# Up products of six FFNs: one 512-column matmul for the high weights, and the weight splits moved between the steps of the hidden part

## The chip, the cores and the metric

The kernel runs on one core of a Trainium2 chip. The metric is the device time of one execution in microseconds (us), as the median of the runs. TensorE (PE in the profile) multiplies, VectorE (DVE) and ScalarE (ACT) work elementwise, SyncE (SP) issues the DMAs. Every engine takes its own instructions in the order in which they are written, and waits on semaphores where one needs what another engine makes.

## The reference, cut to what matters

The program is a small network on 256 tokens of width 1024: two blocks with a mixer and a convolutional FFN each, then two layers with an FFN, a mixer and another FFN. The six FFNs are what the change touches:

```python
def swiglu(h, w_gate, w_up, w_down):
    return (jax.nn.silu(h @ w_gate) * (h @ w_up)) @ w_down
# second block, per layer i
mod = (cond @ w_mod[i] + b_mod[i]).reshape(-1, N_SUBLAYERS, 3, D_MODEL)
h = modulate(x, norm_g[i, 0], mod[:, 0, 0], mod[:, 0, 1])
x = x + FFN_RES_WEIGHT * mod[:, 0, 2][:, None, :] * swiglu(h, ...)
```

The first two FFNs are of another form (`conv_ffn`): the gate half goes through a depthwise convolution of three taps and a gelu before it multiplies the value half. Everything is float32.

## The kernel before, in words

**Precision by parts.** A float32 matrix product is made of three products of rounded operands: each operand is split into a high part (the value rounded to the type that TensorE takes, `fp32r`) and a low part (the rest), and high x high, high x low and low x high are summed. `PASSES` lists the three. A split of a weight piece of 128x1024 is a copy on ACT (high part) and a subtraction on DVE (low part).

**An FFN** (`ffn`, L942) walks over NF = 22 chunks j of 128 hidden channels. The weights of a chunk (two pieces for the up product, gate and value, and one for the down product, 1536 KB in all) come by one DMA into one of four ring slots (`weights`, `load`, L401). `split_up` (L986) splits the two up pieces into the buffer `wu[j % 2]`, `split_down` (L1010) splits the third and then gives the ring slot back. `up_zero` (L1092, chunk 0) and `pe_up` (L1111) make the up product: 2 halves x 8 k-steps x 3 passes = 48 matmuls of 256 columns (the 256 tokens) into one PSUM bank. `hidden` makes gate times value from it: in the plain FFNs silu (L1145, ACT), multiplication (L1172), high part (L1176), low part (L1177, DVE); in the convolutional ones a copy (L1150), the first tap (L1151), two more taps on DVE (L1157) and a gelu (L1166) stand in front. `pe_down` (L1127) multiplies the hidden chunk with the down weights: 12 matmuls of 512 columns.

**Order on TensorE**: up(j), down(j-1), up(j+1), down(j), ... without a gap in the code; down(j-1) waits for `hid[j-1]`, up(j) for the two up splits of chunk j and for the bank that chunk j-2 leaves.

**Modulation columns.** The vector `mod` (144 columns of 128 values) is computed along the way, beside the FFNs: for column c, 512 KB of `w_mod` come by DMA into one of four buffers (`mod_weights`, L981), DVE multiplies them with `crow` (`mod_products`, L1032), ACT sums over the row (`mod_sums`, L1043). When the sum of column c is made, its buffer is free, and the DMA of column c+4 is issued. `due` deals the columns out over chunks 2 to 21: the convolutional FFNs have 17 columns each (at most one in a chunk), the first plain FFN 38, the next two 36 each (two in most chunks, one in the others: 2 and 4 chunks of 20), the last none. The DMAs of weights and of columns stand in one queue, SP's.

**The loop** (`run`) writes, for chunk j: `weights(j+3)`, `split_up(j)`, `pe_up(j)`, `hidden(j-1)`, `mod_products(j)` (in the convolutional FFNs this stands inside `hidden`, after the taps), `mod_sums(j-1)`, `pe_down(j-1)`, `split_down(j)`. The product of column c thus stands behind `hidden(j-1)` on DVE, and the sum of it one turn later.

Of the kernel before, what the change touches and what calls it, by code (L numbers as in the profile page):

```python
# [246 lines left out]
def build(nc, dram, out, pat, cat):  # L247
    V, A, E, G = nc.vector, nc.scalar, nc.tensor, nc.gpsimd
    ctx = ExitStack()
    with ctx:  # L250
# [202 lines left out]
        PASSES = ((0, 0), (0, 1), (1, 0))  # L453
        THIRDS = ((0, slice(0, D)), (1, slice(0, 512)), (1, slice(512, D)))
# [487 lines left out]
        def ffn(name, gain, shift, conv=None, row=None, gate=None, mods=range(0)):  # L942
# [18 lines left out]
            hf = [htok_[:, 4 * T:5 * T]] * 2 if c3 else cv  # L961
            gp = [htok_[:, 5 * T + 4 + q * (T + 4):6 * T + 6 + q * (T + 4)] for q in range(2)]

            slot, up_split, down_split, up, down, mult, hid, mod_in, mod_prod = {}, {}, {}, {}, {}, {}, {}, {}, {}

# [17 lines left out]
            def split_up(j, free):  # L983
                s, full = slot[j]

                @block.scalar  # L986
                def _(_e):
                    A.wait_ge(*full)
                    for point in free:
                        A.wait_ge(*point)  # L990
                for g in range(2):
                    part = slice(g * CHUNK, (g + 1) * CHUNK)
                    raw = slot_ap(s, SLOT)[:, part]

                    @block.scalar
                    def _(_e):
                        Ring.p = act.count(A.activation(wu[j % 2][:, 0, part], raw, ACT.Copy).then_inc(act.sem, 1))  # L997

                    @block.vector
                    def _(_e):  # L1000
                        V.wait_ge(*full)
                        V.wait_ge(*Ring.p)
                        up_split[j, g] = dve.count(V.tensor_tensor(wu[j % 2][:, 1, part], raw, whole(wu[j % 2][:, 0, part]),  # L1003
                                                                   ALU.subtract).then_inc(dve.sem, 1))
# [76 lines left out]
            def up_zero(h_pts):  # L1081
# [3 lines left out]
                @block.tensor  # L1085
                def _(_e):
                    E.wait_ge(*up_split[0, 1])
                    for k in range(KC):
                        E.wait_ge(*h_pts[k])
                        for g in range(2):  # L1090
                            for n_, (wa, ha) in enumerate(PASSES):
                                ins = E.matmul(bank(4 + 2 * g)[:, 0:T], w[:, wa, g, k, :], h[:, ha, k, :],  # L1092
                                               start=k + n_ == 0, stop=k == KC - 1 and n_ == 2)
                    up[0] = pe.count(ins.then_inc(pe.sem, 1))

            def pe_up(j, row_point):

                w = wu[j % 2].rearrange("p a (c k n) -> p a c k n", c=2, k=KC)
                b = bank(4 + j % 2)

                @block.tensor
                def _(_e):
                    if j >= 2:
                        E.wait_ge(*mult[j - 2])
                    elif gate is not None:
                        E.wait_ge(*row_point)
                    for g in range(2):
                        E.wait_ge(*up_split[j, g])
                        for k in range(KC):
                            for n_, (wa, ha) in enumerate(PASSES):  # L1110
                                ins = E.matmul(b[:, g * T:(g + 1) * T], w[:, wa, g, k, :], h[:, ha, k, :],  # L1111
                                               start=k + n_ == 0, stop=k == KC - 1 and n_ == 2)
# [23 lines left out]
            def hidden(j, step):  # L1136

                z = j % 2
                gate_in = bank(4 + z)[:, 0:T]
                value = bank(6)[:, 0:T] if j == 0 else bank(4 + z)[:, T:2 * T]  # L1140
                if not c3:
                    @block.scalar
                    def _(_e):
                        A.wait_ge(*up[j])
                        Ring.p = act.count(A.activation(sg[z], gate_in, ACT.Silu).then_inc(act.sem, 1))  # L1145
                else:
                    @block.scalar
                    def _(_e):
                        A.wait_ge(*up[j])
                        al(A.activation(gp[z][:, 2:T + 2], gate_in, ACT.Copy).then_inc(act.sem, 1))  # L1150
                        Ring.p = act.count(A.activation(cv[z], gp[z][:, 0:T], ACT.Identity, scale=one(f"conv_w{conv}0", j),  # L1151
                                                        bias=one(f"conv_b{conv}", j)).then_inc(act.sem, 1))
                    for tap in (1, 2):
                        @block.vector
                        def _(_e):
                            V.wait_ge(*Ring.p)
                            Ring.p = dve.count(V.scalar_tensor_tensor(cv[z], gp[z][:, tap:tap + T], one(f"conv_w{conv}{tap}", j),  # L1157
                                                                      cv[z], ALU.mult, ALU.add).then_inc(dve.sem, 1))

                    tapped = Ring.p  # L1160
                    mod_products(step)

                    @block.scalar
                    def _(_e):
                        A.wait_ge(*tapped)
                        Ring.p = act.count(A.activation(sg[z], cv[z], ACT.Gelu_apprx_tanh).then_inc(act.sem, 1))  # L1166

                @block.vector
                def _(_e):
                    V.wait_ge(*Ring.p)  # L1170
                    V.wait_ge(*up[j])
                    mult[j] = vl(V.tensor_tensor(hf[z], sg[z], value, ALU.mult).then_inc(dve.sem, 1))  # L1172
                    if 2 <= j < NF - 1:
                        V.wait_ge(*down[j - 2, 1])
                    to = hr[z if j < NF - 1 else 2]
# [4 lines left out]
            def run(h_pts, nxt):  # L1180
# [17 lines left out]
                for j in range(1, NF):  # L1198
# [4 lines left out]
                    if j >= 2:  # L1203
# [2737 lines left out]
```

## Time and profile before

| | |
|---|---|
| median of 3 runs | 1964.86 us (1964.74 to 1965.02) |
| span of the profiled execution | 1963.3 us, first to last instruction; no device time of its own is shown for it |
| PE busy | 1866.7 us, 95% |
| DVE busy | 1426.9 us, 73% |
| ACT busy | 1174.4 us, 60% |
| PE's share of the chain that ended last | 83% |
| of it in up and down products of the FFNs (L1111, L1127, L1092) | 37% + 17% + 2% |

The FFNs lie at about 199 to 386 us, 571 to 758, 769 to 950, 1252 to 1440, 1446 to 1636 and 1770 to 1958. A row of the timeline gives start, duration and engine; "x48" means that so many instructions are merged into the row, and the duration runs from the first start to the last end. In brackets stands how long the engine was idle before it and who released it. The start of one row and of the next on the same engine give the pace; the end of a matmul is modelled and overlaps the next one.

### The profile page before, as it was taken

The page shows a single profiled execution, that of the slowest core. Times are in us where ns is not written, and L with a number is a line of the kernel's source. Part 1 is how long each engine was busy: PE and PEld are TensorE (multiplying, and loading weights), DVE is VectorE, ACT ScalarE, POOL GpSimd, SP SyncE. Part 2 cuts the span into 40 slices and gives each one's busy share as a digit, 9 for nine tenths or more (in the row PEclk, how much of TensorE's full clock was granted, in tenths as well). Part 3 has the DMA queues.
Part 4 walks back from the last instruction along what each step waited for, and adds up shares of the span by engine and source line. Part 5 has one row for each costly group of instructions (what it writes and reads, how often), then busy time and mean ns, then how long its engine had stood idle before and what let it go on. Part 6 is the DMA issues. An engine that isn't in the chain of part 4 may idle for free.

```text
span 1963.3 us, 36008 instructions
## 1 busy us (share of the span) xinstructions
PE 1866.7 (95%) x14638; PEld 1719.9 (88%) x14638; DVE 1426.9 (73%) x2196; ACT 1174.4 (60%) x2092; POOL 12.8 (1%) x25
## 2 busy tenths in 40 slices
PE   7898999898989999999999989999999999999998
PEld 7887999887779998999889967899989998879998
DVE  5687877764677777878778776878787787576555
ACT  6544666664666566666676675666666666575432
POOL 0000000020000000000000000000000000000000
PEclk9999999999999999999999999999999999999999
DMA  8304566354047664888444402588858883224551
GB/s 330 119 4 152 206 236 238 124 192 175 15 196 251 236 211 177 313 301 307 152 149 162 171 2 75 230 304 295 300 212 301 296 286 120 103 97 169 186 193 54
DMA packets 96357, 374.98 MB, mean 191 GB/s; under 512 B 5824, under 2 KB 6464, under 8 KB 95424
## 3 DMA queue, kind: packets, MB, share of 16 engines
q1 hardware_dynamic: 95552, 372.15, 52.5%
q8 instruction: 116, 1.90, 0.4%
q10 hardware_dynamic: 640, 0.52, 0.1%
q14 instruction: 49, 0.40, 0.1%
HBM read 371.08 MB, written 1.05 MB: 190 GB/s over the span
## 4 chain that ended last, share of the span: by engine, by line
PE 83%; DVE 9%; ACT 5%; issue 2%; ACTq 0%; DMA 0%; DVEq 0%; SPq 0%
PE psum L1111 37%; PE psum L1127 17%; PE psum L789 9%; PE psum L882 4%; PE psum L1092 2%; DVE buf L676 1%; PE psum L1742 1%; PE psum L3135 1%; PE psum L745 1%; DVE htok L3026 1%; PE psum L3594 1%; DVE x_res L535 1%; DVE htok L534 1%; PE psum L2628 1%; ACT buf L670 1%
## 5 line engine op out<-in xcount | busy, mean ns | idle before, releaser
L1111 PEld LDWEIGHTS psum<-buf,buf 128*128 128x128 f32 x6048 | 741.2, 192 | 8.9
L1111 PE MATMUL psum<-buf,buf 128*128 128x256 f32 x6048 | 744.4, 283 | 0.0
L1127 PE MATMUL psum<-buf,buf 128*128 128x512 f32 x1584 | 381.9, 391 | 0.0
L1127 PEld LDWEIGHTS psum<-buf,buf 128*128 128x128 f32 x1584 | 289.6, 188 | 55.4 <-DVE buf L1177 0.3
L1003 DVE TENSOR_TENSOR buf<-ring,buf 128x1024 fp32r<-128x1024 f32 x264 | 311.0, 1220 | 8.8 <-DVE modT L1059 7.5
L997 ACT ACTIVATE buf<-ring 128x1024 fp32r<-128x1024 f32 x264 | 263.3, 1046 | 0.0
L789 PE MATMUL psum<-buf,buf 128*128 128x256 f32 x1944 | 244.2, 285 | 7.8 <-DVE buf L676 7.3
L789 PEld LDWEIGHTS psum<-buf,buf 128*128 128x128 f32 x1944 | 236.4, 192 | 13.4 <-DVE buf L676 11.8
L1019 DVE TENSOR_TENSOR buf<-ring,buf 128x1024 fp32r<-128x1024 f32 x132 | 161.6, 1224 | 71.8 <-ACT buf L1014 71.8
L1014 ACT ACTIVATE buf<-ring 128x1024 fp32r<-128x1024 f32 x132 | 139.3, 1055 | 78.9 <-PE psum L1127 75.7
L1032 DVE TENSOR_TENSOR buf<-buf,crow 128x1024 f32<-128x1024 f32 x144 | 171.3, 1219 | 0.0
L1145 ACT ACTIVATE htok<-psum 128x256 f32<-128x256 f32 x88 | 33.7, 384 | 228.6 <-PE psum L1111 228.6
L676 DVE TENSOR_TENSOR buf<-ring,buf 128x1024 fp32r<-128x1024 f32 x97 | 119.0, 1235 | 69.7 <-ACT buf L670 62.5
L1043 ACT ACTIVATE buf<-buf 128x1024 f32<-128x1024 f32 x144 | 150.7, 1051 | 0.0
L1172 DVE TENSOR_TENSOR htok<-htok,psum 128x256 f32<-128x256 f32 x132 | 55.3, 419 | 122.6 <-ACT htok L1145 117.8
L882 PE MATMUL psum<-buf,buf 128*128 128x512 f32 x480 | 113.4, 393 | 1.9 <-DVE buf L866 1.0
L882 PEld LDWEIGHTS psum<-buf,buf 128*128 128x128 f32 x480 | 89.0, 188 | 22.0 <-DVE buf L866 1.7
L670 ACT ACTIVATE buf<-ring 128x1024 fp32r<-128x1024 f32 x97 | 101.7, 1053 | 7.2 <-issue 4.1
L1157 DVE SCALAR_TENSOR_TENSOR htok<-htok,params 128x256 f32<-128x256 f32 x88 | 42.6, 485 | 55.5 <-ACT htok L1151 53.9
L602 PE MATMUL psum<-early,htok 128*128 128x128 f32 x160 | 31.9, 357 | 37.8 <-DVE small L585 37.1
L1150 ACT ACTIVATE htok<-psum 128x256 f32<-128x256 f32 x44 | 16.9, 383 | 84.3 <-PE psum L1111 84.3
L3026 DVE SCALAR_TENSOR_TENSOR htok<-htok,params 128x256 f32<-128x256 f32 x128 | 61.9, 484 | 6.8 <-ACT htok L3018 3.3
(431 smaller groups left out, 2017.9 us busy)
## 6 DMA issues: line engine op xcount, KB each, us to landing
ring<-in_w_ffn SPq DMA_DIRECT2D x88, 1536.0 KB, 6.8
buf<-in_w_mod SPq DMA_DIRECT2D x144, 512.0 KB, 4.5
ring<-in_w_conv SPq DMA_DIRECT2D x44, 1536.0 KB, 6.6
ring<-in_w_ssd_in SPq DMA_DIRECT2D x16, 1536.0 KB, 6.6
ring<-in_w_ns_in SPq DMA_DIRECT2D x7, 1536.0 KB, 6.6
ring<-in_w_hy_in SPq DMA_DIRECT2D x6, 1536.0 KB, 14.8
ring<-in_w_ssd_out SPq DMA_DIRECT2D x5, 1536.0 KB, 6.7
ring<-in_w_cmp SPq DMA_DIRECT2D x4, 1024.0 KB, 5.2
```

The costliest lines, as they stand in the source:

```text
L670: Ring.p = act.count(A.activation(parts[:, 0, :], raw, ACT.Copy).then_inc(act.sem, 1))
L676: Ring.p = dve.count(V.tensor_tensor(parts[:, 1, :], raw, whole(parts[:, 0, :]), ALU.subtract).then_inc(dve.sem, 1))
L789: ins = E.matmul(b[:, 0:T], w[:, wa, k, :], h[:, ha, k, :], start=k + n_ == 0, stop=k == KC - 1 and n_ == 2)
L882: ins = E.matmul(acc[:, t, h * 512:(h + 1) * 512], self.parts[:, la, k % 4, t * P:(t + 1) * P], self.wp[self.turns[k]][wa][:, h * 512:(h + ...
L997: Ring.p = act.count(A.activation(wu[j % 2][:, 0, part], raw, ACT.Copy).then_inc(act.sem, 1))
L1003: up_split[j, g] = dve.count(V.tensor_tensor(wu[j % 2][:, 1, part], raw, whole(wu[j % 2][:, 0, part]), ALU.subtract).then_inc(dve.sem, 1))
L1014: Ring.p = act.count(A.activation(wd[j][:, 0, :], raw, ACT.Copy).then_inc(act.sem, 1))
L1019: down_split[j] = dve.count(V.tensor_tensor(wd[j][:, 1, :], raw, whole(wd[j][:, 0, :]), ALU.subtract).then_inc(dve.sem, 1))
L1032: mod_prod[c] = dve.count(V.tensor_tensor(w, w, crow[:, :], ALU.mult).then_inc(dve.sem, 1))
L1043: Ring.mod_last = act.count(A.activation(w, w, ACT.Copy, accum_out=modT[:, c:c + 1]).then_inc(act.sem, 1))
L1111: ins = E.matmul(b[:, g * T:(g + 1) * T], w[:, wa, g, k, :], h[:, ha, k, :], start=k + n_ == 0, stop=k == KC - 1 and n_ == 2)
L1127: ins = E.matmul(acc[:, t, g * 512:(g + 1) * 512], hr[z][:, ha, t * P:(t + 1) * P], wd[j][:, wa, g * 512:(g + 1) * 512], start=j == 0 and ...
```

## The change

1. `both_parts` (new): for each k-step the high weights are loaded once and multiply high and low part of the input in one matmul of 512 columns, which fills a whole bank; a second matmul of 256 columns adds low weights x high input to the bank's second half. It replaces three matmuls of 256 columns in chunks 0 to 20. Chunk 21 keeps the three passes. Gate and value have a bank each now, so two chunks take banks 4 to 7.
2. `sum_parts` (new): ACT copies the second halves of both banks (128x512) to SBUF, DVE adds the first halves (128x512) to it. Silu or the taps read the sum.
3. The high part of the hidden chunk is made by ACT (a copy to `hr`) in place of DVE's cast.
4. `split_up` for chunk j+1 is no longer one block in front of `pe_up`: its halves are dealt out inside `hidden(j-1)`, and `split_down(j)` stands inside it too.
5. `mod_products(j)` stands in front of `hidden(j-1)` for all FFNs.

```diff
+        def both_parts(b, w_high, w_low, h, k):
+            E.matmul(b.rearrange("p (a t) -> p a t", a=2), w_high, h[:, :, k, :], start=k == 0, stop=False)
+            return E.matmul(b[:, T:2 * T], w_low, h[:, 0, k, :], start=False, stop=k == KC - 1)
...
+            def sum_parts(j):
+                z = j % 2
+                high, low = (psum[:, 4 + 2 * z:6 + 2 * z, a * T:(a + 1) * T] for a in range(2))
+                @block.scalar
+                def _(_e):
+                    A.wait_ge(*up[j])
+                    if j >= 2:
+                        A.wait_ge(*mult[j - 2])
+                    low_part[j] = act.count(A.activation(up_sums[z], low, ACT.Copy).then_inc(act.sem, 1))
+                @block.vector
+                def _(_e):
+                    V.wait_ge(*low_part[j])
+                    up_sum[j] = dve.count(V.tensor_tensor(up_sums[z], high, up_sums[z], ALU.add).then_inc(dve.sem, 1))
...
+            def hidden(j, after):
+                sum_parts(j)
+                if j + 2 < NF:
+                    split_half(j + 2, 0, [up[j]])
+                if c3:
+                    conv_taps(j, up_sum[j])
+                    split_down(j + 1, after)
+                    activate(j, cv[z], tapped[j])
+                else:
+                    activate(j, up_sums[z][:, 0, :], up_sum[j])
+                # DVE: mult[j] = activated * value
...
+                if c3:
+                    if j + 2 < NF:
+                        split_half(j + 2, 1, [up[j]])
+                else:
+                    split_down(j + 1, after)
+                # ACT: high part of the product; DVE: low part, hid[j]
...
+                if not c3 and j + 2 < NF:
+                    split_half(j + 2, 1, [up[j]])
...
-                    if j >= 2:
-                        split_up(j, [up[j - 2]])
                     pe_up(j, row_point)
-                    hidden(j - 1, j)
-                    if not c3:
-                        mod_products(j)
+                    mod_products(j)
+                    hidden(j - 1, [] if j == NF - 1 else [down[j - 2, 1]] if j >= 2 else [h_pts[-1]])
                     mod_sums(j - 1)
```

In the rows of the order that follow, `buf_50` is the column buffer, `buf_136` and `buf_137` are the two up-split buffers, `buf_14x` the down splits, `buf_16x` the hidden parts; branches are left out.

DVE, third FFN, a chunk with two columns, before:

```order
L1003 TENSOR_TENSOR buf_136<-ring,buf_136 128x1024 [waits act_done,slot_full2]
L1003 TENSOR_TENSOR buf_136<-ring,buf_136 128x1024 [waits act_done,slot_full2]
L1172 TENSOR_TENSOR htok<-htok,psum 128x256 [waits pe_done,act_done]
L1176 CAST buf_161<-htok 128x256 [waits pe_done,dve_done]
L1177 TENSOR_TENSOR buf_161<-htok,buf_161 128x256 [waits dve_done]
L1032 TENSOR_TENSOR buf_50<-buf_50,crow 128x1024 [waits mod_full2]
L1032 TENSOR_TENSOR buf_50<-buf_50,crow 128x1024 [waits mod_full3]
L1019 TENSOR_TENSOR buf_142<-ring,buf_142 128x1024 [waits act_done]
```

And after the change:

```order
L1041 TENSOR_TENSOR buf_50<-buf_50,crow 128x1024 [waits mod_full0]
L1041 TENSOR_TENSOR buf_50<-buf_50,crow 128x1024 [waits mod_full1]
L1161 TENSOR_TENSOR hT<-psum,hT 128x512 [waits act_done]
L1008 TENSOR_TENSOR buf_136<-ring,buf_136 128x1024 [waits act_done,slot_full0]
L1202 TENSOR_TENSOR htok<-htok,hT 128x256 [waits act_done]
L1028 TENSOR_TENSOR buf_143<-ring,buf_143 128x1024 [waits act_done]
L1219 TENSOR_TENSOR buf_160<-htok,buf_160 128x256 [waits act_done]
L1008 TENSOR_TENSOR buf_136<-ring,buf_136 128x1024 [waits act_done,slot_full0]
L1041 TENSOR_TENSOR buf_50<-buf_50,crow 128x1024 [waits mod_full2]
L1041 TENSOR_TENSOR buf_50<-buf_50,crow 128x1024 [waits mod_full3]
```

The two column products (L1032, now L1041) stood behind the hidden part; now they stand directly ahead of the sum (L1161) with which the hidden part of chunk j-1 begins.

ACT, the same FFN, before:

```order
L1014 ACTIVATE buf_142<-ring 128x1024 [waits pe_done]
L997 ACTIVATE buf_137<-ring 128x1024
L997 ACTIVATE buf_137<-ring 128x1024
L1145 ACTIVATE htok<-psum 128x256 [waits pe_done]
L1043 ACTIVATE buf_50,modT<-buf_50 128x1024 [waits dve_done]
L1043 ACTIVATE buf_50,modT<-buf_50 128x1024 [waits dve_done]
```

And after the change:

```order
L1156 ACTIVATE hT<-psum 128x512 [waits dve_done,pe_done]
L1002 ACTIVATE buf_137<-ring 128x1024 [waits pe_done,slot_full3]
L1184 ACTIVATE htok<-hT 128x256 [waits dve_done]
L1023 ACTIVATE buf_142<-ring 128x1024 [waits pe_done]
L1214 ACTIVATE buf_161<-htok 128x256 [waits pe_done,dve_done]
L1002 ACTIVATE buf_137<-ring 128x1024 [waits pe_done,slot_full3]
L1052 ACTIVATE buf_50,modT<-buf_50 128x1024 [waits dve_done]
L1052 ACTIVATE buf_50,modT<-buf_50 128x1024 [waits dve_done]
```

The two row sums (L1043, now L1052), which release the DMAs of the columns four further on, stood right behind the silu; now they are the last work of the turn, behind a down split, the copy of the hidden part and the second up split.

## Rows read from the trace of the kernel before

**Rows 1.** The page's first part: busy time, share of the span, instructions.
```profile
PE 1866.7 (95%) x14638; PEld 1719.9 (88%) x14638; DVE 1426.9 (73%) x2196; ACT 1174.4 (60%) x2092; POOL 12.8 (1%) x25
```

**Rows 2.** The page's costliest groups: the matmuls of the FFN products, idle before them last.
```profile
L1111 PE MATMUL psum<-buf,buf 128*128 128x256 f32 x6048 | 744.4, 283 | 0.0
L1127 PE MATMUL psum<-buf,buf 128*128 128x512 f32 x1584 | 381.9, 391 | 0.0
```

**Rows 3.** Timeline, chunks of the first FFN: start, duration, engine, line, count, [idle before].
```profile
252.92 2.91 PE L1127 MATMUL psum<-buf,buf 128*128 128x512 f32 x12
253.12 0.39 ACT L1150 ACTIVATE htok<-psum 128x256 f32<-128x256 f32 x1 [2.10 <-PE psum L1111]
...
255.67 5.92 PE L1111 MATMUL psum<-buf,buf 128*128 128x256 f32 x48
...
261.42 0.86 PE L1127 MATMUL psum<-buf,buf 128*128 128x512 f32 x3
```

**Rows 4.** Timeline, one chunk of the third FFN, two modulation columns in it.
```profile
832.31 1.05 ACT L1043 ACTIVATE buf<-buf 128x1024 f32<-128x1024 f32 x1
...
833.35 1.05 ACT L1043 ACTIVATE buf<-buf 128x1024 f32<-128x1024 f32 x1
833.47 1.37 SPq L981 DMA_DIRECT2D buf<-in_w_mod  x2
833.57 2.35 DVE L1032 TENSOR_TENSOR buf<-buf,crow 128x1024 f32<-128x1024 f32 x2
...
835.74 1.99 ACT L997 ACTIVATE buf<-ring 128x1024 fp32r<-128x1024 f32 x2
...
837.01 2.35 DVE L1003 TENSOR_TENSOR buf<-ring,buf 128x1024 fp32r<-128x1024 f32 x2
837.12 0.38 SPq L401 DMA_DIRECT2D ring<-in_w_ffn  x1
...
842.07 2.35 DVE L1032 TENSOR_TENSOR buf<-buf,crow 128x1024 f32<-128x1024 f32 x2
```

**Rows 5.** DMAs of modulation weights in the first FFN, issue to landing.
```profile
DMA to landing us min/median/max: 3.4/3.5/4.2
```

**Rows 6.** The same in the third FFN.
```profile
DMA to landing us min/median/max: 3.8/4.9/6.5
```

**Rows 7.** Groups by line and shape: operations like the added ones.
```profile
L1157 DVE SCALAR_TENSOR_TENSOR htok<-htok,params 128x256 f32<-128x256 f32 x88 | 42.6, 485 | 55.5 <-ACT htok L1151 53.9
...
L1166 ACT ACTIVATE htok<-htok 128x256 f32<-128x256 f32 x44 | 18.4, 419 | 49.2 <-DVE htok L1157 49.2
...
L3768 ACT ACTIVATE htok<-psum 128x512 f32<-128x512 f32 x16 | 8.8, 619 | 3.7 <-PE psum L3757 3.7
...
L1912 DVE TENSOR_TENSOR buf<-buf,psum 128x512 f32<-128x512 f32 x10 | 6.9, 688 | 3.4 <-PE psum L1742 3.4
```

**Rows 8.** Timeline, start of the first FFN.
```profile
204.66 5.92 PE L1111 MATMUL psum<-buf,buf 128*128 128x256 f32 x48
204.94 1.06 ACT L1014 ACTIVATE buf<-ring 128x1024 fp32r<-128x1024 f32 x1 [1.18 <-DVE htok L1189]
...
206.03 1.22 DVE L1019 TENSOR_TENSOR buf<-ring,buf 128x1024 fp32r<-128x1024 f32 x1 [1.28 <-ACT buf L1014]
```

**Rows 9.** Timeline, start of the third FFN.
```profile
775.07 5.92 PE L1111 MATMUL psum<-buf,buf 128*128 128x256 f32 x48
...
776.90 1.22 DVE L1019 TENSOR_TENSOR buf<-ring,buf 128x1024 fp32r<-128x1024 f32 x1 [1.83 <-ACT buf L1014]
```

**Rows 10.** Windows: length, busy time of each engine, granted clock, DMA share, GB/s.
```profile
204.00:386.00 182.00, 182.00 (x1279) 170.86 (x1278) 141.51 (x204) 112.80 (x172) 0.00 (x0) 1.00 0.59 211
774.00:950.00 176.00, 176.00 (x1256) 166.34 (x1255) 141.27 (x174) 110.70 (x163) 0.00 (x0) 1.00 0.83 292
514.00:519.00 5.00, 3.04 (x26) 2.23 (x23) 4.30 (x10) 2.95 (x11) 0.00 (x0) 1.00 0.00 0
519.00:522.40 3.40, 3.40 (x16) 3.30 (x17) 1.47 (x4) 3.03 (x11) 0.00 (x0) 0.50 0.00 0
```

More of the change, by code:

```diff
@@ L1090, in _ @@
                         for g in range(2):
-                            for n_, (wa, ha) in enumerate(PASSES):
-                                ins = E.matmul(bank(4 + 2 * g)[:, 0:T], w[:, wa, g, k, :], h[:, ha, k, :],
-                                               start=k + n_ == 0, stop=k == KC - 1 and n_ == 2)
+                            ins = both_parts(bank(4 + g), w[:, 0, g, k, :], w[:, 1, g, k, :], h, k)
                     up[0] = pe.count(ins.then_inc(pe.sem, 1))
@@ new lines, in conv_taps, with _ @@
+            def conv_taps(j, point):
+                z = j % 2
+                @block.scalar
+                def _(_e):
+                    A.wait_ge(*point)
+                    Ring.p = act.count(A.activation(cv[z], gp[z][:, 0:T], ACT.Identity, scale=one(f"conv_w{conv}0", j),
+                                                    bias=one(f"conv_b{conv}", j)).then_inc(act.sem, 1))
+                for tap in (1, 2):
+                    @block.vector
+                    def _(_e):
+                        V.wait_ge(*Ring.p)
+                        Ring.p = dve.count(V.scalar_tensor_tensor(cv[z], gp[z][:, tap:tap + T], one(f"conv_w{conv}{tap}", j),
+                                                                  cv[z], ALU.mult, ALU.add).then_inc(dve.sem, 1))
+                tapped[j] = Ring.p
@@ L1142, in _, with hidden_last @@
+            def hidden_last(j):
+                z, to = j % 2, hr[2]
+                gate_in, value = (bank(4 + 2 * z + g)[:, 0:T] for g in range(2))
+                if c3:
                     @block.scalar
@@ L1144, in _ @@
                         A.wait_ge(*up[j])
[L1145 to L1166 removed]
+                        A.wait_ge(*mult[j - 2])
+                        Ring.p = act.count(A.activation(gp[z][:, 2:T + 2], gate_in, ACT.Copy).then_inc(act.sem, 1))
+                    conv_taps(j, Ring.p)
+                    activate(j, cv[z], tapped[j])
+                else:
+                    activate(j, gate_in, up[j])
                 @block.vector
                 def _(_e):
[L1170 removed]
+                    V.wait_ge(*activated[j])
                     V.wait_ge(*up[j])
                     mult[j] = vl(V.tensor_tensor(hf[z], sg[z], value, ALU.mult).then_inc(dve.sem, 1))
[L1173 to L1175 removed]
                     vl(V.tensor_copy(to[:, 0, :], hf[z]).then_inc(dve.sem, 1))
```

76 lines of the change are left out of this document (48 added, 28 removed).

## The prediction

> **What bounds the kernel now.** Read first the busy times: TensorE works 95% of the span, DVE 73%, ACT 60% [rows 1]. Then the groups of the FFN matmuls: 6048 of 256 columns and 1584 of 512, with no idle time before either [rows 2]. Then two timelines. In the first FFN one down product starts at 252.92, the up product at 255.67, the next down product at 261.42 [rows 3]: a turn of 8.50 us, 5.75 for 48 matmuls (0.120 each) and 2.75 for 12 (0.229 each), and nothing between. In the third FFN the two column products start at 833.57 and again at 842.07, the same 8.50 [rows 4]. So TensorE alone sets the pace of all six FFNs, and DVE and ACT follow with room. The question is whether they still do when their order is changed.
>
> The view that decides is again the timeline of the third FFN, read for one buffer [rows 4]: the row sums on ACT start at 832.31 and 833.35, the two column DMAs (one merged row) begin at 833.47, the products that need them start at 842.07. Between issue and use lie 7 to 8 us, and a landing takes 4.9 in the median there [rows 6]. That distance is what the change removes.
>
> **TensorE's part.** Three matmuls of 0.120 become one of 512 and one of 256 columns: 0.229 + 0.120 = 0.349 in place of 0.360. Per chunk 16 x 0.349 = 5.58 in place of 5.75: 0.17 us gained, in 21 chunks of each FFN 3.6 us, where TensorE still sets the pace. The 512-column price is that of the down product, whose input is contiguous; here it is two stretches of 256. I take it at the same price, the nearest row. The bounds are 0.240 (twice a matmul of 256, no gain) and 0.218 (twice the 0.109 that 256 further columns add between the two rows): 0 to 0.35 us a chunk, so over the 63 chunks of three FFNs in which TensorE still sets the pace 0 to 22 us, where I take 11.
>
> The row gives 0.120 for 256 columns at the full clock. The Trainium skill (TensorE: Matmul & The Clock Gate, "Wait — 56ns, not 53.3ns?") has start to start as columns over 2.4 GHz plus about 2.5 ns, 109 ns for 256 columns; by it a merged pair saves 2.5 ns, 0.04 us a chunk, and the total would come out some 9 us higher. The trace disagrees on the level (120, not 109), and I go by the trace.
>
> **What is added outside.** ACT copies 128x512 from PSUM: 0.62, the price of L3768; DVE adds 128x512 with PSUM: 0.69, that of L1912 [rows 7]. The high part of the hidden chunk goes from DVE to ACT (0.42, as L1166). As a load this is bearable: two DVE instructions of 128x1024 start 1.13 apart (2.35 for two of 1.22 [rows 4]), so DVE has per turn of a plain FFN five of these (three splits, two columns), 5.65, the sum 0.60, product and low part 0.33 each: 6.9 us of 8.33 (5.58 + 2.75). Between the two bounds (none hidden, 1.3 us a turn, 160 us; all hidden) I take all hidden as far as load goes, since TensorE needs the hidden part only a turn later.
>
> **The new loop, in the three FFNs with 36 or 38 columns.** DVE now takes the products of chunk j ahead of the sum of chunk j-1, and ACT makes the row sums last in the turn. The product of column c+4 waits for a DMA that waits for the row sum of column c, and with two columns a chunk that sum stands at the end of the turn just before. Everything of the hidden part is queued behind the waiting product on DVE: sum, splits, multiplication, low part; down(j-1) waits for them. Laid out from the start of the sum (0):
> - sum 0.69; the first up split starts at 0.60, the multiplication at 1.73 and ends at 2.15 (the silu, from 0.73, is long done).
> - ACT: high part from 2.19, second up split from 2.52, first row sum from 3.46 (two ACT copies of 128x1024 take 1.99, so they start 0.95 apart [rows 4]). From a row sum's start to its DMA 1.16 (832.31 to 833.47), the second 1.04 later [rows 4]: DMAs at 4.62 and 5.66.
> - Landing: 3.4 to 4.2, median 3.5, where the queues are little loaded [rows 5], 4.9 where they are at 83% [rows 6, 10]. The longer turn takes load away, and the 1536 KB of weights, which go out right behind the columns (now at 837.12, after a wait for the down split [rows 4]), have nine us to land. I take 3.6 for the first, 3.8 for the second.
> - First product at 8.27, second at 5.66 + 3.8 + 0.05 = 9.51, next sum 1.13 later: a turn of 10.64.
> - Where only the first of the two DMAs is waited for (a chunk with one column lies between, which shifts the distance), the product starts at 8.27 and the turn is 9.40.
>
> TensorE needs 8.33 of such a turn; it waits ahead of down(j-1), for the low part. Against 8.50 before, a full turn costs 2.14, a partial one 0.90. Dealing out the columns: the first two chunks with columns use the DMAs issued ahead; of the other 18 chunks of the 38-column FFN 14 turns are full and 4 partial, of each 36-column FFN 8 and 10. So 30 x 2.14 + 24 x 0.90 = 64.2 + 21.6 = 85.8 us. The slack of the first such turn (the low part would be ready some 2.5 us early) is lost again at the end, where the last down products follow each other without an up product between; I enter neither. The bounds of this term: zero if the wait never comes last; with every landing at the 4.9 of rows 6, 1.1 more per full and 1.3 more per partial turn, 33 + 31 = 64 us more; with 3.4 for all, some 14 less.
>
> The Trainium skill (DMA: Bandwidth & Descriptors, "Anatomy of one DMA") has a fixed part of about 2.0 us and 436 GB/s behind it, written for GpSimd's path: 3.2 us for 512 KB, an estimate. By it the total would be some 24 us lower. The shortest landing in these rows is 3.4, so I stay above.
>
> **The starts.** up(1) is over 5.58 after its start, and down(0) has no other product ahead of it. First FFN: up(1) starts at 204.66, DVE takes the down split of chunk 0 from 206.03 [rows 8]; the sum can start at 207.16, then split, two taps (0.48 each [rows 7]), down split, multiplication, and split and low part behind it: 0.60 + 1.13 + 1.0 + 1.13 + 0.33 + 1.13 + 0.43 = 5.75, ready at 212.9, against 210.2: 2.7 lost, in two FFNs. Third FFN: 775.07 and 776.90 [rows 9]; the sum from 778.03, then 0.60 + 1.13 + 0.33 + 1.13 + 0.43 = 3.6, ready at 781.65 against 780.65: 1.0 lost, in four FFNs. In the convolutional FFNs there is at most one column a chunk, so column c+4 is due four or more chunks after c, and the loop doesn't close. Their later turns stay with TensorE: DVE has 4 x 1.13 + 0.60 + 1.0 + 0.66 = 6.8 of 8.33.
>
> **Sum.** Loops +85.8; starts 2 x 2.7 + 4 x 1.0 = +9.4; gain 3 x 3.6 in the two convolutional FFNs and the last = -10.8; 3 x 3 chunks ahead of the loops x 0.17 = -1.5. Together +82.9: 1963.3 + 82.9 = 2046.2 us of span. The median of the runs is 1.6 above the profiled span; so 2048.
>
> **Rivals.**
> - Faster: the loop never closes, because the columns' data are there before DVE asks, and only the starts remain: 6 x 3.6 = 21.6 less, 9.4 more: 1963.3 - 12.2 + 1.6 = 1953. For it: 7 to 8 us between issue and use now [rows 4]. Against: the order on both engines, which leaves less than nothing of them. It decides from landings under 1.5 us, where a full turn (6.84 plus the landing) falls below TensorE's 8.33. Chance 0.09.
> - Slower still: the landings stay at 4.9, as in this FFN now [rows 6], because the weights and the second column share the queues: 2048 + 64 = 2112. Chance 0.08.
> - The clock: in a full turn TensorE stands for 10.64 - 8.33 = 2.3 us. Before, a stretch with 3.04 busy of 5.00 us was followed by 3.40 at clock 0.50, that is 1.2 GHz [rows 10]. One such stretch in a turn costs 1.7 of TensorE's time, inside the 2.3, so nothing. If the clock stays low, a turn needs 16.7, 6.0 and 7.3 over the two turns: 30 x 6.0 + 24 x 7.3 = 355 more, 2400. The Trainium skill (same TensorE page, "HAM oscillation") warns of exactly such waits between bursts; the stretch in rows 10 agrees, at a lower busy share than here. Chance 0.03.
> - In between, the loops closing less tightly (the sums earlier on ACT than laid out): 1965 to 2015, chance 0.06.
>
> **Numbers.** The forecast has 0.74. Range 2015 to 2090: the short landings below, half-way to the long ones above; what is left out is the faster case, the clock, half of the long landings and part of the in-between. A change within 0.2% (3.9 us, about what a measurement of this kernel can tell from none) has 0.02, faster by more 0.10, slower by more 0.88.
>
> **What would show it.** Right: in the third FFN DVE idle ahead of L1041 released by the DMA, about 2 us a turn; TensorE idle ahead of the down product, near 2.3 and 1.1; turns of 10.6 and 9.4; up products of 5.58; landings near 3.6; the convolutional and the last FFN shorter by 1 to 3 us each. Wrong: turns of 8.3 in the third FFN, or DVE waiting elsewhere; up products still at 5.75.

## The result, and the profile after

The changed kernel takes 2114.38 us (median of 4 runs, 2105.75 to 2119.56) against 1964.8: ratio 1.0756 with the interval 1.0738 to 1.0773, slower by 149.6 us. The forecast was 2048 with a range of 2015 to 2090: right in direction and place, too small by 66 us, and outside the range. The rival with the long landings had 2112. Ratios leave out one run, the one of ten of experiment 1 that took 2080.0 us at a granted clock of 0.842.

The page of the changed kernel (busy times, chain by line, and three groups of matmuls beside the column product), to be held against [rows 1, 2]:

```profile
PE 1907.4 (90%) x12622; PEld 1640.4 (78%) x12622; DVE 1468.4 (70%) x2196; ACT 1271.4 (60%) x2302; POOL 12.8 (1%) x25
...
DMA buf<-in_w_mod 12%; PE psum L457 10%; PE psum L1137 9%; PE psum L795 8%; PE psum L458 5%; ACT buf L1052 4%; DVE buf L1008 4%; PE psum L888 4%; ACT buf L1002 3%; DVE hT L1161 2%; DVE buf L682 1%; PE psum L751 1%; PE psum L1803 1%; DVE buf L1028 1%; DVE htok L1202 1%
...
L457 PE MATMUL psum<-buf,buf 128*128 128x512 f32 x2016 | 720.1, 400 | 3.0 <-DVE buf L627 2.9
L458 PE MATMUL psum<-buf,buf 128*128 128x256 f32 x2016 | 566.7, 281 | 0.0
L1137 PE MATMUL psum<-buf,buf 128*128 128x512 f32 x1584 | 420.1, 418 | 102.2 <-DVE buf L1219 100.3
...
L1041 DVE TENSOR_TENSOR buf<-buf,crow 128x1024 f32<-128x1024 f32 x144 | 175.6, 1223 | 213.1 <-DMA buf<-in_w_mod 210.1
```

TensorE has less to do in instructions (12622 matmuls for 14638) and stands idle ahead of the down product for 102 us, where before it never stood [rows 2]. DVE stands ahead of the column product for 213 us, 210 of them released by the columns' DMA, and this DMA has 12% of the chain. The list of who waited for whom (total, times, longest) names the links of one loop:

```profile
ACT htok L1184 <- DVE hT L1161: 280.5, 66, 7.4
DVE buf L1041 <- DMA buf<-in_w_mod: 210.1, 84, 4.6
...
PE psum L1137 <- DVE buf L1219: 100.3, 53, 4.3
```

One full turn of the fifth FFN, in its timeline (compare [rows 4]):

```profile
1699.83 1.04 ACT L1052 ACTIVATE buf<-buf 128x1024 f32<-128x1024 f32 x1
...
1700.10 5.49 PE L1137 MATMUL psum<-buf,buf 128*128 128x512 f32 x12 [4.03 <-DVE buf L1219]
...
1700.87 1.04 ACT L1052 ACTIVATE buf<-buf 128x1024 f32<-128x1024 f32 x1
1700.98 1.37 SPq L990 DMA_DIRECT2D buf<-in_w_mod  x2
...
1702.40 0.43 SPq L401 DMA_DIRECT2D ring<-in_w_ffn  x1
1704.66 1.23 DVE L1041 TENSOR_TENSOR buf<-buf,crow 128x1024 f32<-128x1024 f32 x1 [3.42 <-DMA buf<-in_w_mod]
...
1707.80 1.22 DVE L1041 TENSOR_TENSOR buf<-buf,crow 128x1024 f32<-128x1024 f32 x1 [1.91 <-DMA buf<-in_w_mod]
...
1708.95 0.68 DVE L1161 TENSOR_TENSOR hT<-psum,hT 128x512 f32<-128x512 f32 x1
...
1710.68 0.42 DVE L1202 TENSOR_TENSOR htok<-htok,hT 128x256 f32<-128x256 f32 x1
...
1711.13 0.42 ACT L1214 ACTIVATE buf<-htok 128x256 fp32r<-128x256 f32 x1
...
1712.21 0.42 DVE L1219 TENSOR_TENSOR buf<-htok,buf 128x256 fp32r<-128x256 f32 x1
1712.40 1.04 ACT L1052 ACTIVATE buf<-buf 128x1024 f32<-128x1024 f32 x1
...
1712.68 2.55 PE L1137 MATMUL psum<-buf,buf 128*128 128x512 f32 x10 [1.04 <-DVE buf L1219]
...
1713.56 1.37 SPq L990 DMA_DIRECT2D buf<-in_w_mod  x2
```

Read it from the row sums: ACT sums at 1699.83 and 1700.87, the column DMAs go out from 1700.98, the weights at 1702.40; DVE waits 3.42 us for the first column and 1.91 for the second; its sum (L1161) starts at 1708.95. Counted from there, the multiplication starts 1.73 later, the high part 2.18, the next row sum 3.45 and the next column DMA 4.61 later. The forecast had 1.73, 2.19, 3.46 and 4.62. The engines' part of the loop was right to 0.01 us. TensorE waits ahead of both down products (4.03 and 1.04).

What was wrong is one landing. The DMAs of the two columns in this turn, issued at 1700.98 and 1702.02, first and second:

```profile
L990 SPq DMA_DIRECT2D buf<-in_w_mod x1: 328/328/328, 1701.0 to 1701.0; - x1
...
DMA to landing us min/median/max: 3.7/3.7/3.7
```

```profile
L990 SPq DMA_DIRECT2D buf<-in_w_mod x1: 328/328/328, 1702.0 to 1702.0; - x1
...
DMA to landing us min/median/max: 5.8/5.8/5.8
```

Over the three FFNs 46 pairs of columns 1 us apart land in 3.69 us (first) and 5.56 us (second) in the mean; the forecast had 3.6 and 3.8. By the forecast a full turn is 6.84 plus the landing of the second, so 12.40 with this mean. From one DVE sum (L1161) to the next, as the forecast laid it out, 30 turns are above 10.7, 12.41 in the mean, and each of the 30 is the landing of its own second column plus 6.82 or 6.83. From one down product's start to the next, as turns are given in what follows, those above 10.7 have 12.28.

Windows over the third and the fifth FFN, one down product of the third, and the last FFN (length, busy, granted clock, DMA share and GB/s as in [rows 10]):

```profile
772.02:1020.50 248.48, 204.78 (x984) 168.52 (x985) 157.46 (x187) 136.45 (x217) 0.00 (x0) 0.93 0.61 212
1552.51:1780.73 228.22, 199.27 (x983) 165.40 (x984) 154.67 (x185) 134.55 (x213) 0.00 (x0) 0.95 0.63 221
863.20:866.60 3.40, 3.40 (x9) 2.64 (x9) 0.16 (x1) 2.34 (x4) 0.00 (x0) 0.51 0.73 193
1919.12:2105.00 185.88, 184.71 (x983) 158.03 (x984) 111.87 (x140) 93.66 (x137) 0.00 (x0) 1.00 0.43 153
```

The granted clock is at its lower level, 1.2 GHz, in stretches of the down products that follow a wait (0.51 in the third row); in the last FFN, with no columns, it is at 2.4 GHz throughout (1.00).

### The profile page after: what moved, and what is told of

Same layout as the page of the kernel before. It is cut to its first block, busy times and chain, and to the rows that moved or that the text cites. A ratio compares the mean times of both kernels' runs of the same rounds, so it can differ in the third digit from the quotient of the medians.

```text
span 2110.8 us, 32184 instructions
## 1 busy us (share of the span) xinstructions
PE 1907.4 (90%) x12622; PEld 1640.4 (78%) x12622; DVE 1468.4 (70%) x2196; ACT 1271.4 (60%) x2302; POOL 12.8 (1%) x25
## 4 chain that ended last, share of the span: by engine, by line
PE 50%; DVE 18%; ACT 13%; DMA 12%; issue 6%; ACTq 0%; DVEq 0%; SPq 0%
DMA buf<-in_w_mod 12%; PE psum L457 10%; PE psum L1137 9%; PE psum L795 8%; PE psum L458 5%; ACT buf L1052 4%; DVE buf L1008 4%; PE psum L888 4%; ACT buf L1002 3%; DVE hT L1161 2%; DVE buf L682 1%; PE psum L751 1%; PE psum L1803 1%; DVE buf L1028 1%; DVE htok L1202 1%
## 5 line engine op out<-in xcount | busy, mean ns | idle before, releaser
L457 PE MATMUL psum<-buf,buf 128*128 128x512 f32 x2016 | 720.1, 400 | 3.0 <-DVE buf L627 2.9
L458 PE MATMUL psum<-buf,buf 128*128 128x256 f32 x2016 | 566.7, 281 | 0.0
L1137 PE MATMUL psum<-buf,buf 128*128 128x512 f32 x1584 | 420.1, 418 | 102.2 <-DVE buf L1219 100.3
L457 PEld LDWEIGHTS psum<-buf,buf 128*128 128x128 f32 x2016 | 381.9, 189 | 99.0 <-DVE buf L627 6.2
L1137 PEld LDWEIGHTS psum<-buf,buf 128*128 128x128 f32 x1584 | 307.8, 201 | 186.7 <-DVE buf L1219 117.9
L458 PEld LDWEIGHTS psum<-buf,buf 128*128 128x128 f32 x2016 | 383.2, 190 | 5.0
L1008 DVE TENSOR_TENSOR buf<-ring,buf 128x1024 fp32r<-128x1024 f32 x264 | 321.4, 1221 | 20.2 <-ACT buf L1002 19.2
L1041 DVE TENSOR_TENSOR buf<-buf,crow 128x1024 f32<-128x1024 f32 x144 | 175.6, 1223 | 213.1 <-DMA buf<-in_w_mod 210.1
L1002 ACT ACTIVATE buf<-ring 128x1024 fp32r<-128x1024 f32 x264 | 275.5, 1049 | 0.0
L795 PE MATMUL psum<-buf,buf 128*128 128x256 f32 x1944 | 245.5, 286 | 7.5 <-DVE buf L682 7.1
L795 PEld LDWEIGHTS psum<-buf,buf 128*128 128x128 f32 x1944 | 237.7, 193 | 13.1 <-DVE buf L682 11.6
L1184 ACT ACTIVATE htok<-hT 128x256 f32<-128x256 f32 x84 | 34.9, 415 | 280.5 <-DVE hT L1161 280.5
L1028 DVE TENSOR_TENSOR buf<-ring,buf 128x1024 fp32r<-128x1024 f32 x132 | 161.8, 1225 | 28.2 <-ACT buf L1023 26.5
L1023 ACT ACTIVATE buf<-ring 128x1024 fp32r<-128x1024 f32 x132 | 139.0, 1053 | 48.5 <-PE psum L1137 45.5
L682 DVE TENSOR_TENSOR buf<-ring,buf 128x1024 fp32r<-128x1024 f32 x97 | 118.6, 1231 | 69.8 <-ACT buf L676 62.6
L1156 ACT ACTIVATE hT<-psum 128x512 f32<-128x512 f32 x126 | 74.0, 587 | 134.8 <-PE psum L458 132.5
L1052 ACT ACTIVATE buf<-buf 128x1024 f32<-128x1024 f32 x144 | 150.1, 1044 | 0.0
L1161 DVE TENSOR_TENSOR hT<-psum,hT 128x512 f32<-128x512 f32 x126 | 86.7, 688 | 87.0 <-ACT hT L1156 87.0
L888 PE MATMUL psum<-buf,buf 128*128 128x512 f32 x480 | 113.3, 393 | 1.9 <-DVE buf L872 1.0
L888 PEld LDWEIGHTS psum<-buf,buf 128*128 128x128 f32 x480 | 89.0, 188 | 21.9 <-DVE buf L872 1.7
L676 ACT ACTIVATE buf<-ring 128x1024 fp32r<-128x1024 f32 x97 | 101.6, 1053 | 6.9 <-issue 3.8
```

The costliest lines, as they stand in the source:

```text
L457: E.matmul(b.rearrange("p (a t) -> p a t", a=2), w_high, h[:, :, k, :], start=k == 0, stop=False)
L458: return E.matmul(b[:, T:2 * T], w_low, h[:, 0, k, :], start=False, stop=k == KC - 1)
L682: Ring.p = dve.count(V.tensor_tensor(parts[:, 1, :], raw, whole(parts[:, 0, :]), ALU.subtract).then_inc(dve.sem, 1))
L795: ins = E.matmul(b[:, 0:T], w[:, wa, k, :], h[:, ha, k, :], start=k + n_ == 0, stop=k == KC - 1 and n_ == 2)
L888: ins = E.matmul(acc[:, t, h * 512:(h + 1) * 512], self.parts[:, la, k % 4, t * P:(t + 1) * P], self.wp[self.turns[k]][wa][:, h * 512:(h + ...
L1023: Ring.p = act.count(A.activation(wd[j][:, 0, :], raw, ACT.Copy).then_inc(act.sem, 1))
```

## The experiments

All times are against the kernel before on the same chip, 1964.6 to 1965.1.

**1. The products behind the hidden part again.**

```diff
                     pe_up(j, row_point)
-                    mod_products(j)
+                    if c3:
+                        mod_products(j)
                     hidden(j - 1, [] if j == NF - 1 else [down[j - 2, 1]] if j >= 2 else [h_pts[-1]])
+                    if not c3:
+                        mod_products(j)
```

> The changed kernel with one edit: in the plain FFNs the column products stand behind the hidden part on DVE again, as before the change; all else of the change stays. Theory (a closed loop: row sum, column DMA, product, sum, hidden part, row sum, holds the three FFNs with 36 or 38 columns): the loop has a whole turn more of slack, the waits of DVE for the column DMAs (210 us in the changed kernel) go to nearly nothing, every FFN turn is 8.39 us, and the time falls by some 155 us to 1955-1963, a little below the kernel before. Rival (it is the added load on DVE and ACT, or the clock that falls to half, that makes the turns long): the time stays above 2050.

Measured: 1965.66 us, ratio 1.000 (0.9984 to 1.0016). A turn of the third FFN:

```profile
855.27 1.37 SPq L990 DMA_DIRECT2D buf<-in_w_mod  x2
...
855.59 2.36 DVE L1041 TENSOR_TENSOR buf<-buf,crow 128x1024 f32<-128x1024 f32 x2
...
857.33 2.91 PE L1137 MATMUL psum<-buf,buf 128*128 128x512 f32 x12
```

DVE takes the two products right after their predecessor, without a wait, and TensorE starts the down product without one. The turns of the plain FFNs are 8.39, but for a first one of up to 8.49. The loop is the whole loss: with the rest of the change in place, this one place is worth 149 us. The time is 3 us above the expected stretch, so of the gain of the shorter turns nothing is left; experiment 6 looks for it.

**2. The weights held back behind the columns.** `weights(j + 3)` stands behind `mod_products(j)` and its DMA waits for the last of two products:

```diff
+                        if len(due[j]) == 2:
+                            Ring.used[Ring.n % RING] = Ring.used[Ring.n % RING] + [mod_prod[due[j][-1]]]
+                        weights(j + 3)
```

> The changed kernel with one edit: where a chunk has two modulation columns, the 1536 KB DMA of weights for chunk j+3 is issued only when the products of these columns are done, so it no longer goes out 0.4 us behind the second column's DMA. The loop stays closed. Theory (the second column lands late, in 4.8 to 7 us, because the weights share the queues; that is the part of the forecast that was too small): the second landing comes down to 3.6-3.9 us, full turns from about 12.6 to 10.7, partial turns stay at 9.4-9.5, and the time is 2050-2065. Rival (the long full turns come from the half clock in the down products, or from the loop's ACT and DVE part): the landings get shorter but the turns stay above 12, and the time stays above 2095.

Measured: 2102.21 us, ratio 1.0695 (1.0679 to 1.0711). The expectation was missed; the time speaks for the rival, the landings say why:

```profile
1688.11 1.37 SPq L990 DMA_DIRECT2D buf<-in_w_mod  x2
...
1692.87 2.49 DVE L1041 TENSOR_TENSOR buf<-buf,crow 128x1024 f32<-128x1024 f32 x2 [4.50 <-DMA buf<-in_w_mod]
...
1695.28 0.69 DVE L1161 TENSOR_TENSOR hT<-psum,hT 128x512 f32<-128x512 f32 x1
...
1695.43 0.38 SPq L401 DMA_DIRECT2D ring<-in_w_ffn  x1
...
1699.89 1.37 SPq L990 DMA_DIRECT2D buf<-in_w_mod  x2
```

The weights now go out at 1695.43, and 4.46 us later, at 1699.89, the next columns, while they are still arriving (they land at 1702.30). First and second landing are 4.37 and 4.98 in the mean over 46 pairs: the second got shorter by 0.6, the first longer by 0.7, and the partial turns with it. The turns above 10.7 have 11.73, and 6.84 + 4.98 is 11.82. So the turn follows the landing, but the edit only moved the overlap.

**3. The row sums right behind the silu.** `mod_sums` is called behind `activate` in the plain FFNs, with the products left ahead of the hidden part.

> The changed kernel with one edit: in the plain FFNs the two row sums on ACT stand right behind the silu, ahead of the down split, the high part and the second up split; products stay in front of the hidden part. Theory (loop): the column DMAs go out 2.4 us earlier after the sum, so every closed turn gets about 2.4 us shorter: full ones about 10.2, partial ones fall to TensorE's 8.39; the time is 1995-2025. The hidden part comes later by the two sums, up to 2 us, inside the turn. Rival (the columns' place on ACT does not matter because DVE's wait is for bandwidth, not for the issue): no change, 2105-2120.

Measured: 2002.47 us, ratio 1.0181 (1.0154 to 1.0208), inside the expected stretch. In the third FFN the columns go out 1.48 us after the silu's start, and the products find them landed (in brackets: what DVE waits for now):

```profile
898.32 0.42 ACT L1184 ACTIVATE htok<-hT 128x256 f32<-128x256 f32 x1 [2.49 <-DVE hT L1161]
...
899.80 1.37 SPq L990 DMA_DIRECT2D buf<-in_w_mod  x2
...
901.80 1.23 DVE L1028 TENSOR_TENSOR buf<-ring,buf 128x1024 fp32r<-128x1024 f32 x1 [2.05 <-ACT buf L1023]
...
904.41 2.35 DVE L1041 TENSOR_TENSOR buf<-buf,crow 128x1024 f32<-128x1024 f32 x2
```

The loop can be opened from its ACT side too: DVE's waits for the columns' DMA fall from 210.1 us to 4.8. The turns did not come as expected, though (10.2 full, 8.39 partial): they are 8.4 to 10.2, with 9.1 the most frequent. With the two sums ahead of it, ACT's copy for the down split comes later, and DVE now waits for that (136.1 us in all, 26.5 in the changed kernel). That the total fell inside the expected stretch is partly luck.

**4. The two parts of the input next to each other**, on top of experiment 1:

```diff
-            return Region(at).take(2 * n * T, F32R).rearrange("p (a k t) -> p a k t", a=2, k=n)
+            return Region(at).take(2 * n * T, F32R).rearrange("p (k a t) -> p a k t", a=2, k=n)
```

> The kernel with the column products behind the hidden part, and in addition the two parts of the input lie next to each other for each k-step, so that the 512 columns of the merged matmul are one contiguous stretch. Theory A (the merged matmul takes 0.236 us start to start and not 0.229 because its input is read in two stretches 8 KB apart): it falls to 0.227-0.229, the pair from 0.353 to 0.346, and the time by 126 chunks x 16 x 0.007 = 14 us against the same kernel without this. Theory B (the input's layout does not matter, the pace is set by something else, such as the two weight loads per pair or VectorE and ScalarE at work beside it): pair at 0.353 and the same time within 3 us.

Measured: 1965.36 us, ratio 1.0004 (0.9989 to 1.0019), and turns of 8.39 as without it. Theory B: that the 512 columns are read in two stretches costs nothing that can be seen.

**5. A third of the weights' bytes**, from chunk 4 on in the three FFNs. Two of the three pieces of a chunk are left out, so the outputs are not the network's.

> The changed kernel, but in the three FFNs with 36 or 38 columns the weight DMAs of chunks 4 to 21 bring only one of three pieces (512 KB in place of 1536), so their results are made from stale weights; every instruction of the engines is the same. Theory (a full turn is 6.84 us plus the landing of the second column, and that landing is 5.6 instead of the forecast 3.8 because the weights follow it on the same queues; holding them back only moved the overlap to the next columns): first landing 3.5-3.6, second 3.7-4.2, full turns 10.6-11.0, and the time 2050-2065, close to the forecast of 2048. Rival (the second landing is slow because it follows the first column by 1 us, or the rest of the turn is longer than laid out): second landing stays above 5, time above 2090.

Measured: 2101.25 us, ratio 1.0693 (1.0679 to 1.0708). The rival's numbers: first landing 3.58, second 5.35, turns above 10.7 at 12.15 (6.84 + 5.35 = 12.19). But a 512 KB DMA still goes out 0.4 us behind the second column, so it was open whether the follower or the first column delays the second. Experiment 8 parts them.

**6. Chunk 0 first**, on top of experiment 1: `split_down(0)` stands behind the multiplication of chunk 0, and `split_half(2, ...)` and `split_down(1)` behind its low part; `weights(4)` is written behind them.

```diff
-                split_down(0, [h_pts[-1]])
...
+                if j == 0:
+                    split_down(0, after)
...
+                if j == 0:
+                    split_half(2, 0, [up[0]])
+                    split_half(2, 1, [up[0]])
+                    split_down(1, after)
```

> The kernel with the column products behind the hidden part, and in addition another order at the start of each FFN: the hidden part of chunk 0 comes first, and the down splits of chunks 0 and 1 and both up splits of chunk 2 behind or inside it, so that down(0) need not wait. Theory (of the 2.1 us that the shorter turns of 8.39 give in each FFN the late hidden part of chunk 0 takes 1 to 1.1 in a plain and 2.8 to 4.2 in a convolutional one): the plain FFNs come to about 185.0 us from first to last matmul start and the convolutional ones to 185, against 187.07 before; in all 9 to 12 us less than before, 1953-1957, ratio 0.994-0.996. Rival (the start was not the cause; the lost time lies between the stages): no change, 1963-1966.

Measured: 1955.3 us (1954.42 to 1962.05), ratio 0.9955 (0.9941 to 0.9968): 9 us faster than the kernel before, as expected in the total. By stage it is less clear. From first to last matmul start the last FFN has 184.72 (187.07 to 187.44 for such FFNs before, 185.98 in experiment 1), but the third has 185.92 and the convolutional ones 187.6, where 185 was expected: in the first of these down(0) still waits 0.6 and down(1) 1.6; that the splits put off from chunk 0 now delay chunk 1 is a reading that no run tests. The profiled execution took 1962.05 us (span 1960.3): in it the six FFNs together are 5.8 us shorter than before and the rest 2.8 longer, so where the rest of the 9 us lies is not shown.

**7. Filler for TensorE in the wait**, in the turns j = 4 to 20 of the three FFNs.

```diff
+                    if len(mods) > 17 and 4 <= j < NF - 1:
+                        @block.tensor
+                        def _(_e):
+                            E.wait_ge(*up_sum[j - 1])
+                            for _n in range(10):
+                                E.matmul(bank(4 + 2 * ((j + 1) % 2)).rearrange("p (a t) -> p a t", a=2), h[:, 0, 0, 0:P],
+                                         h[:, :, 0, :], start=True, stop=True)
```

> The changed kernel with ten matmuls of 512 columns, whose results nobody reads, put ahead of each down product of the three FFNs with 36 or 38 columns: TensorE does them after the sum of the chunk, in the time in which it would wait for the hidden part. Theory (the fall of the granted clock to 1.2 GHz in some down products is a result of the waits and is hidden in them): the half-clock stretches inside these FFNs go away or become few, the turns stay at 12 and 9.4, and the time stays within 1% of the changed kernel, 2095-2125. Rival (the half clock lengthens the turns): the time falls by 15 us or more below 2098.

Measured: 2114.09 us, ratio 1.0762 (1.0747 to 1.0776), the changed kernel's time. Windows over the third and the fifth FFN:

```profile
775.00:1020.00 245.00, 230.62 (x1152) 190.04 (x1152) 157.26 (x188) 137.05 (x218) 0.00 (x0) 0.99 0.61 215
1557.00:1784.00 227.00, 224.50 (x1155) 189.78 (x1154) 155.02 (x186) 135.03 (x214) 0.00 (x0) 1.00 0.63 223
```

The clock is 0.99 and 1.00 where it was 0.93 and 0.95, and the three FFNs are as long as they were (245, 229 and 227 us from first to last matmul start against 248, 225 and 228). In these three FFNs the half clock was a result of the waits and cost nothing.

**8. Both 2 and 5**, so that in most turns no weights are on the way while two columns land. The edit of 2 holds the weights back only in chunks with two columns, so behind some pairs a DMA still goes out at once: weights in a chunk with one column, or those of the next stage at the end of an FFN.

> The changed kernel with two edits together: the weight DMA of chunk j+3 is issued only behind the products of two columns, and in the three FFNs with 36 or 38 columns it brings one of three pieces for chunks 4 to 21 (their results come from stale weights). Neither alone took the weights off the columns: held back, they still ran when the next columns went out (first landing 4.5, second 4.8); cut to a third, they still went out 0.4 us behind the second column (second landing 5.4). With both, nothing of the weights is in flight while two columns land. Theory (the forecast's loop with its own landings): first landing 3.5-3.6, second 3.7-3.9, full turns 10.6-10.8, time 2050-2065. Rival (two columns 1 us apart delay each other enough on their own): second landing at 4.5 or more, full turns above 11.4, time 2085 or more.

Measured: 2083.54 us, ratio 1.0593 (1.057 to 1.0617), inside neither expectation: 18.5 us above the theory's 2050 to 2065 and just under the rival's 2085, with the landings nearer to the rival's. A turn of the third FFN:

```profile
907.81 1.79 SPq L994 DMA_DIRECT2D buf<-in_w_mod  x2
...
911.56 1.23 DVE L1045 TENSOR_TENSOR buf<-buf,crow 128x1024 f32<-128x1024 f32 x1 [3.49 <-DMA buf<-in_w_mod]
...
914.08 1.23 DVE L1045 TENSOR_TENSOR buf<-buf,crow 128x1024 f32<-128x1024 f32 x1 [1.29 <-DMA buf<-in_w_mod]
...
915.22 0.68 DVE L1165 TENSOR_TENSOR hT<-psum,hT 128x512 f32<-128x512 f32 x1
...
915.38 0.33 SPq L402 DMA_DIRECT2D ring<-in_w_ffn  x1
...
919.84 0.33 SPq L994 DMA_DIRECT2D buf<-in_w_mod  x1
```

The weights of 915.38 are in (at 919.15) when the next column goes out at 919.84. A second column of the fifth FFN, and one of the next pair, behind which weights went out at once:

```profile
L994 SPq DMA_DIRECT2D buf<-in_w_mod x1: 328/328/328, 1671.9 to 1671.9; - x1
...
DMA to landing us min/median/max: 4.4/4.4/4.4
...
1683.51 0.43 SPq L402 DMA_DIRECT2D ring<-in_w_ffn  x1
...
L994 SPq DMA_DIRECT2D buf<-in_w_mod x1: 328/328/328, 1683.1 to 1683.1; - x1
...
DMA to landing us min/median/max: 5.7/5.7/5.7
```

First landing 3.60, second 4.80 in the mean over all 46 pairs; the turns above 10.7 have 11.52 (6.84 + 4.80 = 11.64). The mean mixes two kinds. In 12 pairs another DMA of this queue still goes out 0.37 us behind the second column, and this lands in 5.34; in the other 34 none does within a microsecond, and it lands in 4.61 (median 4.47). So even left alone, two columns 1 us apart cost the second about 1 us more than a lone one (3.6), and the rest of the 5.56, about 1 us too, is the weights behind it.

**9. The kernel before with the products ahead of the hidden part.**

```diff
-                    hidden(j - 1, j)
                     if not c3:
                         mod_products(j)
+                    hidden(j - 1, j)
```

> The kernel before with one edit: in the plain FFNs the column products stand ahead of the hidden part on DVE, as in the changed kernel. The row sums stay right behind the silu on ACT, and the silu waits for the up product alone, not for a sum made by DVE. Theory (the loop needs both: products ahead of the hidden part and row sums behind work of ACT that waits for DVE): the columns' DMAs go out 2 us into the turn, land before DVE comes to the products 8.5 us later or little behind; no closed loop, 1963-1972. Rival (the place of the products alone makes the long turns): full turns of 10 us and more, 2020 or more.

Measured: 1964.98 us, ratio 0.9996 (0.9986 to 1.0006), turns of 8.50 as before. The place of the products alone costs nothing. With experiments 1 and 3 this says that the loop closes where both hold: the products ahead of the hidden part, and ACT's row sums behind work that waits for DVE's sum.

## Why the prediction was right in place and wrong in size

**What bounded the kernel** and the distance between issue and use of a column held: given back in experiment 1, it takes all of the loss away.

**The loop's engine part** was laid out to within 0.02 us, and the partial turns came as forecast (9.40; most of them are 9.3 to 9.7 in the fourth and fifth FFN). The count came too: from sum to sum 14, 8 and 8 turns are above 10.7 and 4, 10 and 10 below. That there are full and partial ones, with the 38-column FFN the longest, came as forecast too (248.5 us from first to last matmul start against 225.4 and 228.2).

**The failed step: "I take 3.6 for the first, 3.8 for the second."** The first was 3.69, the second 5.56. 30 full turns at 12.4 in place of 10.64 are 53 us, of the 66 that were missing. The reason given for 3.8 was that the longer turn takes load off the queues. It does (a DMA share of 0.61 to 0.63 against 0.83 [rows 10]), but the share is a mean over the turn, and the two columns and the weights go out within 1.4 us of each other, once a turn. Of the 1.76 us missing, about 0.8 is the pair itself (4.61 without the weights, experiment 8) and about 1.0 the weights behind it. The price was also taken from the wrong rows: the columns of [rows 5] go out one by one, at least 8.49 us apart, while in the third, fourth and fifth FFN of the kernel before none of 46 second columns landed in under 4.15 us (mean 5.00). Experiments 2, 5 and 8 together show that the turn is 6.84 plus this landing whatever makes it: 11.82, 12.19 and 11.64 worked out, 11.73, 12.15 and 11.52 measured. Why a column lands later with another 1 us ahead of it, or with a DMA 0.4 us behind it, stays open.

The rival of the long landings had named half of this (the weights and the second column share the queues) and priced it by [rows 6] at 2112. That it came within 2.4 us is luck. It lengthened the partial turns too, by 24 x 1.3 = 31 us, which did not happen, and had the full turns too short (11.74 against 12.4, 30 x 0.66 = 20 us); another 11 us, outside these loops, it did not have either.

**Sum of the three FFNs**: forecast +87 us (85.8 + 3.0 - 1.5), measured +141 (702.1 against 561.2 from first to last matmul start). Two side sums of the prediction are off, and neither is in the forecast: with 3.4 for all landings the term is 17 us less (30 x 0.4 + 24 x 0.2), not 14, and with 3.2 it is 28 less, not 24.

**TensorE's part.** The pair of matmuls was priced at 0.349 and takes 0.353 ((8.39 - 2.75) / 16): turns are 8.39 where 8.33 was forecast, a gain of 0.11 in place of 0.17 per turn. The last FFN gained 1.5 us for 2.6. The layout of the input is not the reason (experiment 4); what makes the pair 4 ns longer than its two prices is open. The rule of the Trainium skill weighed in the forecast (TensorE: Matmul & The Clock Gate, "Wait — 56ns, not 53.3ns?": columns over 2.4 GHz plus about 2.5 ns) would have made the gain 0.04 by an estimate, and the measured one lies between. Its level, by estimate 325 ns for the pair, is again not what the turns show (353).

**The starts.** Forecast 2.7 us of loss less 3.6 of gain in a convolutional FFN; measured +2.2 in the first and +0.7 in the second. In the first of them the first turn has 9.99 us and the other 8.49: after the wait for the hidden part of chunk 0 (2.09 and 2.62 us) the down product took 4.34 us in one, with the granted clock at 0.68 to 0.72, and 3.01 in the other, at 1.00. Whether it falls varies from profile to profile (in experiment 1 it is the second FFN that has 9.93 and the first 8.53), and with it 1.5 us.

**Of the rest** 5 us lie between the FFNs (before the fifth FFN 1.6, before the last 2.6, after the third 0.7); no run was made for them.

**The clock rival** fell as argued: half clock in some down products (0.93 to 0.95 in the mean), hidden in the waits of the three FFNs, shown by experiment 7. The faster rival fell with the order on the two engines. What experiment 1 gives is not what that rival had (1953); it took experiment 6 to come near.

## What to carry to other kernels

When work is moved ahead on an in-order queue, look for what it waits for and follow that back once round: if the release comes from another engine's last work of the turn, and this work waits for the first engine, a loop closes, and its length (here 6.84 us of engines and one landing) replaces the bound there was. Price the landing in such a loop by what is issued within a microsecond of it, not by the queues' mean share, and take the price from rows with the same neighbours. A fallen clock beside a wait need not be what costs the time: filler work in the wait tells. In the three loops it cost nothing, in the first turn of a convolutional FFN 1.5 us.

## What the runs showed of the hardware that was not expected

- Two DMAs of 512 KB issued 1.04 us apart from one queue, with no other of that queue in the microsecond behind them, land in 3.60 and 4.61 us in the mean (experiment 8, 34 pairs; a lone one in 3.6). With 1536 KB issued 0.4 us behind the second in nearly all pairs they land in 3.69 and 5.56 (the changed kernel, 46 pairs), with 512 KB in 3.58 and 5.35 (experiment 5). Here that something follows matters more than its size.
- A 512-column matmul whose input lies in two stretches 8 KB apart keeps the pace of one with a contiguous input: turns of 8.39 us both ways.
